# Second and third branch product of a hybrid trunk step as three rounded products each

## The chip, the core and the metric

The kernel runs on one core of one Trainium2 chip, as one program. The core has five engines that run side by side and meet through semaphores: TensorE (PE, matmul; its weight loads have a row of their own, PEld), VectorE (DVE), ScalarE (ACT), GpSimd (POOL) and SyncE (SP), whose work here is to issue DMAs. The metric is the device time of one execution in microseconds, as the median over runs of the whole program.

## What is computed

One step of a hybrid trunk for 384 tokens (128 context, 256 latent) of width 1024. Each layer normalizes and modulates the tokens, projects them, runs three branches on the projections (attention A, gated convolution B, a recurrence C), mixes them, and then runs a mixture of 64 experts. The reference, cut to the part that matters here:

```python
(qa, ka, va, u, gb, gc, qc, zf, zb, ic, oc, ga, gbr, gcr) = jnp.split(n @ lp['w_in'], split_idx, axis=-1)
o_a = attend(heads(qa), ka, va)
o_b = conv_branch(u, gb, gc, lp['w_conv'])
o_c, s_f, s_b = hgrn_branch(qc, zf, zb, ic, oc, lp['lb_f'], lp['lb_b'], lp['hgrn_g'], s0f, s0b)
mix = (jax.nn.sigmoid(ga) * (o_a @ lp['w_br_a'])
       + jax.nn.sigmoid(gbr) * (o_b @ lp['w_br_b'])
       + jax.nn.sigmoid(gcr) * (o_c @ lp['w_br_c'])) @ lp['w_out']
h = h + g1 * mix
n2 = rmsnorm(h, lp['norm2_g']) * (1 + sc2) + sh2
y = moe(n2.reshape(bsz * t, D_MODEL), lp).reshape(bsz, t, D_MODEL)
```

Each branch output is 384 x 512 and its weight 512 x 1024; all values are float32.

## The kernel before

One list, `SCHEDULE`, sets the order of the work in each engine: every engine walks the same list of stages and emits its own part of each. Semaphores between the engines do the rest. The stages run roughly in this order: norm and modulation; the input projection in units of 128 output columns (`unit`); attention between those units; the recurrence (`gates`, `decays`, `sums`, `ops`, `level`, `carry`); its outputs (`hout`, `ho_sq`, `ho_norm`, `hout_t`), with the first four branch products between them; the other 20 branch products (`branches`); the output projection (`wout`); the second norm; router, shared expert and table; and last the routed experts in a loop, 40 units here.

**Branch products.** There are 24, numbered i = 0 to 23: 8 for each branch (`br, j = i // KD, i % KD`). Product i gives 128 output columns for all 384 tokens, transposed, from 4 blocks of 128 inputs. It is made by `product` (line 1614), which emits 4 f32 matmuls with the weight block as the stationary operand (128x128) and the branch output as the moving one (128x384). An f32 matmul leaves two records in the trace, so a product leaves 8. The sources are `OA` (branch A), `GB` (B) and `OCT` (C). Products 0 to 3 stand between the recurrence's output stages, and `branches` runs 4 to 23. The results go to PSUM banks in turn, six of them from product 8 on, and TensorE waits only for the taking of product i - 6.

**Takings.** VectorE takes product i out of PSUM and multiplies it by its gate (`G`, line 1383); for branches B and C it then adds it to the sum of the first (line 1386). At i = 8 it first does three small additions for the gate rows (lines 1374 to 1376). The output projection waits for the last addition (`mix_done`).

**Recurrence outputs.** For m = 0 to 2 ScalarE copies the output (`hout`, line 863), VectorE sums its squares (lines 1340 to 1342), ScalarE takes a root (line 870), VectorE scales (lines 1068 to 1072, 1349), TensorE transposes (`hout_t`, line 1823) and VectorE writes `OCT` (line 1361).

**Weights.** SyncE streams them through a ring of three slots (`bigA`). The three branch weights have a slot each; the two halves of the output weights follow when the products of branch A and of branch B are done (lines 593 and 603).

**Rounded products.** The input projection already works with the form that the change uses. ScalarE copies a weight piece to a rounded high part (`split`, line 789, of 128x2048; `split_g`, line 781, of 128x1024), VectorE subtracts it from the whole and writes the low part over the weight in the ring (lines 1173 and 1142), and TensorE makes high x high, high x low and low x high (lines 1664 to 1666 and 1676 to 1678). A rounded matmul leaves one record. A unit has 8 blocks and 24 such matmuls, and ScalarE takes it at line 763.

**Memory.** `GB`, `OCT`, `KEY`, `QC` and `Z` are stretches of one tile, `bigB`; `nT` holds the low part of the normalized tokens (`NLO`) until the last unit. GpSimd clears the rows that the expert gathers will fill, a memset of 128x2048 on `bigB` (line 1017), when `ho_ready` says that the recurrence's outputs are in PSUM; the gathers come after the second norm.

## Time and profile before

| | us |
|---|---|
| median of the runs | 1142.43 |
| lowest and highest of three runs | 1141.66, 1144.81 |
| profiled execution, its own time | 1142.93 |
| its span in the trace | 1141.0 |
| TensorE busy | 1077.7 (94%) |
| VectorE busy | 449.1 (39%) |
| ScalarE busy | 296.3 (26%) |
| GpSimd busy | 131.4 (12%) |

The profile is one execution, recorded on the chip. Its times count from the span's start; the own time is what the device reports for that execution, 1.9 us more than the span. Busy time of TensorE counts pipelined matmuls with their modelled ends, so their durations overlap; how fast matmuls follow each other is read from the distance between starts, or from when another engine takes the results. "Idle before" and what stands behind the arrow say how long the engine had nothing to do ahead of an instruction and which work ended that.

### The profile page before, as it was taken

What the parts mean: (1) busy time and instruction counts of PE and PEld (TensorE: products, weight loads), DVE (VectorE), ACT (ScalarE), POOL (GpSimd) and SP (SyncE); (2) the same over time, 40 slices, a digit from 0 to 9 for tenths busy, and PEclk for the clock granted to TensorE, in tenths of its full rate; (3) what the DMA queues carried; (4) which work ended last, traced back from release to release, by engine and by line L of the source; (5) the groups of instructions that cost most, each with busy time, mean ns of one, the idle gap of its engine ahead of it and who ended that gap; (6) DMA issues with size and microseconds to landing.
All of it is one profiled execution on the core that took longest, in us unless ns stands there. A gap on an engine that the chain in (4) does not pass through costs nothing.

```text
span 1141.0 us, 14556 instructions
## 1 busy us (share of the span) xinstructions
PE 1077.7 (94%) x4704; PEld 671.6 (59%) x4704; DVE 449.1 (39%) x1046; ACT 296.3 (26%) x439; POOL 131.4 (12%) x142
## 2 busy tenths in 40 slices
PE   4999999998999988999999999999999999999985
PEld 2499988787888985554645444444444444444432
DVE  2233544355789837334641212211212212211247
ACT  3334443337444444001321111111111111111101
POOL 0020321000000000000015111121111121121100
PEclk9999999999999999999998999999999999999998
DMA  9999875447444333540239999999999999999683
GB/s 355 398 257 371 118 96 87 149 166 269 176 149 148 149 135 92 179 147 1 93 161 413 369 394 385 404 395 377 385 414 391 378 380 409 408 394 387 257 357 156
DMA packets 88527, 306.60 MB, mean 269 GB/s; under 512 B 13398, under 2 KB 17750, under 8 KB 66464
## 3 DMA queue, kind: packets, MB, share of 16 engines
q1 hardware_dynamic: 68896, 270.63, 60.6%
q0 software_dynamic: 12256, 26.80, 10.2%
q10 hardware_dynamic: 7328, 8.55, 2.2%
q8 instruction: 29, 0.48, 0.2%
q14 instruction: 18, 0.15, 0.0%
HBM read 285.31 MB, written 36.85 MB: 282 GB/s over the span
## 4 chain that ended last, share of the span: by engine, by line
PE 35%; DMA 20%; issue 4%; DVE 4%; ACT 1%; POOLq 1%; POOL 0%; ACTq 0%; DVEq 0%
DMA y_parts<-bigB,IDX 17%; PE PS L1614 10%; PE PS L1951 6%; PE PS L1953 4%; PE PS L1968 3%; DMA bigB<-n_rows,IDX 3%; PE PS L1937 2%; PE PS L2019 2%; PE PS L1970 2%; PE PS L1908 1%; PE PS L2027 1%; PE PS L1676 1%; PE PS L1678 0%; PE PS L1677 0%; PE PS L1986 0%
## 5 line engine op out<-in xcount | busy, mean ns | idle before, releaser
L1951 PE MATMUL PS<-bigB 128*128 128x512 f32 x224 | 103.9, 608 | 0.0
L1664 PE MATMUL PS<-bigB_r 128*128 128x384 f32 x288 | 98.7, 343 | 3.2 <-ACT bigB L763 1.9
L1666 PE MATMUL PS<-bigB_r,bigA_r 128*128 128x384 f32 x288 | 96.5, 335 | 0.0
L1665 PE MATMUL PS<-nT_r,bigB_r 128*128 128x384 f32 x288 | 96.3, 334 | 0.0
L1953 PE MATMUL PS<-bigA,bigB 128*64 128x512 f32 x208 | 94.8, 598 | 0.0
L1954 PE MATMUL PS<-bigB 128*64 128x512 f32 x208 | 94.8, 598 | 0.0
L1951 PE MATMUL PS<-bigA,bigB 128*128 128x512 f32 x208 | 94.6, 597 | 0.0
L1551 DVE TENSOR_SCALAR bigB<-PS,bigD 128x1024 f32<-128x1024 f32 x40 | 51.3, 1283 | 101.5 <-PE PS L1968 68.9
L939 ACT ACTIVATE bigB<-PS 128x1024 f32<-128x1024 f32 x40 | 41.0, 1025 | 158.4 <-PE PS L1937 158.4
L1173 DVE TENSOR_TENSOR bigA_r<-bigA,bigB_r 128x2048 fp32r<-128x2048 f32 x18 | 41.3, 2292 | 98.2 <-ACT bigB_r L789 98.1
L1529 DVE TENSOR_TENSOR bigB<-bigB,PS 128x256 f32<-128x256 f32 x40 | 16.9, 421 | 158.1 <-ACT bigB L943 158.1
L1012 POOL DMA_INDIRECT bigB<-n_rows,IDX x27 | 27.4, 1016 | 407.1 <-issue 376.7
L1951 PEld LDWEIGHTS PS<-bigB 128*128 128x128 f32 x224 | 41.4, 194 | 42.5 <-issue 42.5
L1678 PE MATMUL PS<-bigC_r,bigA_r 128*128 128x384 f32 x192 | 65.0, 338 | 0.0
L763 ACT ACTIVATE bigB<-PS 128x384 f32<-128x384 f32 (+1 forms) x55 | 27.3, 497 | 144.3 <-PE PS L1666 70.8
L1090 DVE TENSOR_REDUCE bigD<-PS 128x1 f32<-128x2 f32 (+1 forms) x58 | 9.2, 158 | 139.1 <-PE PS L1623 122.2
L1664 PEld LDWEIGHTS PS<-bigB_r 128*128 128x128 f32 x288 | 54.0, 188 | 9.6 <-ACT bigB L763 3.7
L1951 PEld LDWEIGHTS PS<-bigA,bigB 128*128 128x128 f32 x208 | 37.6, 191 | 37.3 <-issue 37.3
L1614 PE MATMUL PS<-bigA,bigB 128*128 128x512 f32 x120 | 52.9, 596 | 3.4 <-ACT bigB L933 2.2
L1665 PEld LDWEIGHTS PS<-nT_r,bigB_r 128*128 128x128 f32 x288 | 54.1, 188 | 0.0
L1666 PEld LDWEIGHTS PS<-bigB_r,bigA_r 128*128 128x128 f32 x288 | 54.0, 188 | 0.0
L1953 PEld LDWEIGHTS PS<-bigA,bigB 128*64 128x64 f32 x208 | 26.3, 136 | 46.3 <-issue 44.5
(352 smaller groups left out, 1901.3 us busy)
## 6 DMA issues: line engine op xcount, KB each, us to landing
bigA<-in_w_in SPq DMA_DIRECT2D x17, 2048.0 KB, 11.7
bigB<-in_w_gate SPq DMA_DIRECT2D x27, 1024.0 KB, 9.3
bigB<-in_w_up SPq DMA_DIRECT2D x27, 1024.0 KB, 12.5
bigB<-in_w_down SPq DMA_DIRECT2D x27, 1024.0 KB, 12.6
bigA<-in_w_gate SPq DMA_DIRECT2D x26, 1024.0 KB
bigA<-in_w_up SPq DMA_DIRECT2D x26, 1024.0 KB
bigA<-in_w_down SPq DMA_DIRECT2D x26, 1024.0 KB, 11.0
bigA<-in_w_ada SPq DMA_DIRECT2D x8, 2048.0 KB, 10.0
```

What stands on the lines that cost most here:

```text
L939: nc.scalar.activation(XT[:, b, :, :].rearrange("p (a k) t -> p a (k t)", a=2), PS[:, 0:2, :], ACT.Copy).then_inc(xt_done, 1)
L1173: nc.vector.tensor_tensor(low, w, WHI[:, i % 2, :, :].bitcast(F32), ALU.subtract).then_inc(wlo_done, 1)
L1551: nc.vector.tensor_scalar(YS[:, p % 2, :].rearrange("p (a n) -> p a n", a=2), PS[:, 6:8, :], WC[:, p:p + 1], None, ALU.mult).then_inc(ys_d ...
L1614: last = mm(out, lhs(k), rhs(k), start=(k == 0), stop=(k == n - 1))
L1664: mm(out, wh, nh, start=(k == 0), stop=False)
L1665: mm(out, wh, nl, start=False, stop=False)
L1666: last = mm(out, wl, nh, start=False, stop=(k == KD - 1))
L1678: last = mm(out, low[:, k, :], NHI2[:, k, :], start=False, stop=(k == KD - 1))
L1951: last = mm(PS[:, 2 + b, :], XT[:, b, k, :], GU_W[s][:, :, k, :], start=first, stop=stop)
L1953: mm(PS[0:HALF, 2 + b, :], XT[:, b, k, 0:HALF], GU_W[2][:, :, k, :], start=first, stop=stop)
L1954: last = mm(PS[HALF:P, 2 + b, :], XT[:, b, k, HALF:P], GU_W[3][:, :, k, :], start=first, stop=stop)
L1968: last = mm(PS[:, 6 + hf, :], HT[:, b, k, :], DN_W[s][:, k, cols], start=(k == 0), stop=(k == 1))
```

## The change

The 16 products of branches B and C are made from rounded parts: 12 rounded matmuls each in place of 4 f32 ones. Products 0 to 7 and the output projection stay f32. The operands are split as follows.

- Sources: ScalarE copies `GB` and `OCT` (128x1536 each) to `SRC_H`, in `nT`; VectorE writes the low part over the source itself (`SRC_L`).
- Weights: each of the two branch weights is split in four pieces of 4 x 256 columns (two products each), 8 pieces in all. ScalarE copies a piece to `BRH`, over `KEY`, `QC` and `Z` (pieces 0 to 6) and over `GB`'s place (piece 7, which waits for all 16 products of branches A and B); VectorE writes the low part over the piece in the ring.
- `LATE_LOW_AT` says after which product's taking VectorE makes which low part. The stage `late_high` places ScalarE's copies.
- GpSimd's memset on `bigB` now waits for all 24 products, since pieces 3 and 4 lie there.

```diff
+LATE = ([("src", 1)] + [("br", i) for i in range(4)] + [("src", 2)] + [("br", i) for i in range(4, 8)])
+LATE_LOW_AT = {4: [("src", 1), ("br", 0)], 5: [("br", 1)], 6: [("br", 2)], 7: [("br", 3)], 9: [("src", 2)],
+               10: [("br", 4)], 12: [("br", 5)], 14: [("br", 6)], 16: [("br", 7)]}
...
-    s += [("carry_t",), ("late_sig",), ("carry_products",), ("br", 0), ("br", 1), ("hout", 0), ("brm", 0), ("brm", 1),
+    s += [("carry_t",), ("late_sig",), ("late_high", "src", 1), ("carry_products",), ("br", 0), ("br", 1), ("hout", 0), ("brm", 0), ("brm", 1),
...
-    s += [("late_act", b) for b in range(3)]
-
-    s += [("gates_out",), ("branches",), ("mod2",), ("wout", 0, 0), ("wout", 0, 1), ("norm2", 0), ("wout", 1, 0),
+    s += [("late_high", "br", 0), ("late_high", "br", 1), ("late_act", 0), ("late_act", 1), ("late_high", "br", 2),
+          ("late_high", "br", 3), ("late_high", "src", 2)] + [("late_high", "br", i) for i in range(4, 7)]
+    s += [("late_act", 2), ("gates_out",), ("late_high", "br", 7), ("branches",), ("mod2",), ("wout", 0, 0), ("wout", 0, 1), ("norm2", 0), ("wout", 1, 0),
...
+        SRC_H = [None, cut(nT_r, 0, (4, T)), cut(nT_r, 4 * T, (4, T))]
+        SRC_L = [None, cut(bigB_r, 15360, (4, T)), cut(bigB_r, 13824, (4, T))]
+        BRH = [cut(bigB_r, 16896 + 1024 * i, (4, 2 * P)) for i in range(7)] + [cut(bigB_r, 15360, (4, 2 * P))]
...
+        def late_part(key):
+
+            kind, i = key
+            if kind == "src":
+                return (GB, OCT)[i - 1], SRC_H[i], SRC_L[i]
+            cols = slice(i % 4 * 2 * P, (i % 4 + 1) * 2 * P)
+            at = SLOT_OF["br", 1 + i // 4] % NSLOT * 4096
+            whole, low = (t[:, at:at + 4096].rearrange("p (k n) -> p k n", k=4) for t in (bigA, bigA_r))
+            return whole[:, :, cols], BRH[i], low[:, :, cols]
...
+                elif st == "late_high":
+                    kind, i = ev[1:]
+                    if kind == "src":
+                        if i == 1:
+                            act.wait_ge(unit_ready, len(UNITS))
+                            act.wait_ge(conv_done, 4)
+                        else:
+                            act.wait_ge(hot_taken, NT)
+                        whole, high, _ = late_part(ev[1:])
+                        nc.scalar.activation(high, whole, ACT.Copy).then_inc(late_high, 1)
+                    else:
+                        arrived(act, ("br", 1 + i // 4))
+                        act.wait_ge(kh_done, 4)
+                        if i >= 3:
+                            act.wait_ge(ho_ready, NT)
+                        if i == 7:
+                            act.wait_ge(br_ready, 2 * KD)
+                        whole, high, _ = late_part(ev[1:])
+                        nc.scalar.activation(high, whole, ACT.Copy).then_inc(late_high, 1)
...
-            pool.wait_ge(ho_ready, NT)
+            pool.wait_ge(br_ready, 3 * KD)
             link(nc.gpsimd.memset(bigB[:, 19968:22016], 0.0))
...
+                        for key in LATE_LOW_AT.get(i, ()):
+                            whole, high, low = late_part(key)
+                            dve.wait_ge(late_high, LATE.index(key) + 1)
+                            nc.vector.tensor_tensor(low, whole, high.bitcast(F32), ALU.subtract).then_inc(late_low, 1)
...
-                        src = (OA, GB, OCT)[br]
-                        product(PS[:, br_bank(i), 0:T], lambda k: w[:, k, j * P:(j + 1) * P], lambda k: src[:, k, :], 4).then_inc(br_ready, 1)
+                        out = PS[:, br_bank(i), 0:T]
+                        if br == 0:
+                            product(out, lambda k: w[:, k, j * P:(j + 1) * P], lambda k: OA[:, k, :], 4).then_inc(br_ready, 1)
+                            continue
+                        piece = (i - KD) // 2
+                        _, high, low = late_part(("br", piece))
+                        pe.wait_ge(late_low, LATE.index(("src", br)) + 1)
+                        pe.wait_ge(late_low, LATE.index(("br", piece)) + 1)
+                        cols = slice(j % 2 * P, (j % 2 + 1) * P)
+                        for k in range(4):
+                            mm(out, high[:, k, cols], SRC_H[br][:, k, :], start=(k == 0), stop=False)
+                            mm(out, high[:, k, cols], SRC_L[br][:, k, :], start=False, stop=False)
+                            last = mm(out, low[:, k, cols], SRC_H[br][:, k, :], start=False, stop=(k == 3))
+                        last.then_inc(br_ready, 1)
```

How the instructions stand on three engines, before and after. TensorE before, from product 2 to the output projection: line 1614 is `product`, 1823 the transposes of the recurrence's output; `bigD` is `OA`'s tile, `bigB` that of `GB` and `OCT`, `bigA` the weights (and, with 512 columns, the output weights).

```order
L1614 MATMUL PS<-bigD,bigA 128x384 x4
L1823 MATMUL PS<-K,bigC 128x128 x4
L1614 MATMUL PS<-bigD,bigA 128x384 x4
L1823 MATMUL PS<-K,bigC 128x128 x4
L1614 MATMUL PS<-bigD,bigA 128x384 x16
L1614 MATMUL PS<-bigB,bigA 128x384 x64
L1614 MATMUL PS<-bigA,bigB 128x512 x32
```

TensorE after, from product 3 into product 8 (1656 and 1865 are the old 1614 and 1823):

```order
L1656 MATMUL PS<-bigD,bigA 128x384 x4
L1865 MATMUL PS<-K,bigC 128x128 x4
L1656 MATMUL PS<-bigD,bigA 128x384 x16
L1893 MATMUL PS<-nT_r,bigB_r 128x384
L1894 MATMUL PS<-bigB_r 128x384
L1895 MATMUL PS<-nT_r,bigA_r 128x384
L1893 MATMUL PS<-nT_r,bigB_r 128x384
L1894 MATMUL PS<-bigB_r 128x384
L1895 MATMUL PS<-nT_r,bigA_r 128x384
```

The 64 f32 matmuls of products 8 to 23 have become 64 triples like these; nothing else on TensorE moved.

VectorE before, products 4 to 9: line 1383 is a taking, 1386 the addition, 1374 to 1376 the gate rows.

```order
L1383 TENSOR_TENSOR bigB<-PS,bigB 128x384 x4
L1374 TENSOR_TENSOR csil<-csil 128x64
L1375 TENSOR_TENSOR csil<-csil 128x32
L1376 TENSOR_TENSOR csil<-csil 128x32
L1383 TENSOR_TENSOR bigB<-PS,bigB 128x384
L1386 TENSOR_TENSOR bigB<-bigB 128x384
```

VectorE after, products 4 to 7 (line 1421 is the taking, 1430 a low part):

```order
L1421 TENSOR_TENSOR bigB<-PS,bigB 128x384
L1430 TENSOR_TENSOR bigB_r<-bigB,nT_r 128x1536
L1430 TENSOR_TENSOR bigA_r<-bigA,bigB_r 128x4x256
L1421 TENSOR_TENSOR bigB<-PS,bigB 128x384
L1430 TENSOR_TENSOR bigA_r<-bigA,bigB_r 128x4x256
L1421 TENSOR_TENSOR bigB<-PS,bigB 128x384
L1430 TENSOR_TENSOR bigA_r<-bigA,bigB_r 128x4x256
L1421 TENSOR_TENSOR bigB<-PS,bigB 128x384
L1430 TENSOR_TENSOR bigA_r<-bigA,bigB_r 128x4x256
L1412 TENSOR_TENSOR csil<-csil 128x64
```

Ten low parts have come in, five of them ahead of product 8's taking and five behind later ones.

ScalarE before, from the last root of the recurrence's output to the gate rows (line 886 is the sigmoids of `G` for branches B and C):

```order
L870 ACTIVATE small<-small 128x4
L878 DMA csil<-ada_rows 128x8x16
L881 DMA bigC<-ada_rows 128x8x8 x2
L882 DMA bigB<-in_x 128x3x1024
L883 DMA csil<-in_b_gate 128x16
L886 ACT_TABLE_LOAD
L886 ACTIVATE bigB<-bigB 128x3072 x2
L891 DMA gate_rows<-csil 64x2x16 x2
L895 DMA bigC<-gate_rows 128x4096
```

ScalarE after, from that root's successor on (924 a piece's high part, 915 a source's, 905 the sigmoids, 929 and 933 the gate rows):

```order
L924 ACTIVATE bigB_r<-bigA 128x1024 x2
L897 DMA csil<-ada_rows 128x8x16
L900 DMA bigC<-ada_rows 128x8x8 x2
L901 DMA bigB<-in_x 128x3x1024
L902 DMA csil<-in_b_gate 128x16
L905 ACT_TABLE_LOAD
L905 ACTIVATE bigB<-bigB 128x3072
L924 ACTIVATE bigB_r<-bigA 128x1024 x2
L915 ACTIVATE nT_r<-bigB 128x1536
L924 ACTIVATE bigB_r<-bigA 128x1024 x3
L905 ACTIVATE bigB<-bigB 128x3072
L929 DMA gate_rows<-csil 64x2x16 x2
```

Two high parts stand ahead of the DMA issues now, six between the sigmoids, one behind the gate rows; a tenth (source 1) stands earlier, right behind the Silu of `late_sig`.

## Rows read from the trace of the kernel before

**Rows 1.** The chain that ended last, 420 to 610 us: start, us, what

```profile
442.30 1.58 DVE small L1342
...
451.92 53.31 PE PS L1614 x160
...
506.46 27.73 PE PS L1614 x64
```

**Rows 2.** Timeline of TensorE: start, us, engine, line, out<-in, count, idle before

```profile
445.97 0.66 PE L1823 MATMUL PS<-K,bigC 128*128 128x128 f32 x4 [1.40 <-DVE bigC L1349]
...
451.29 0.63 PE L1823 MATMUL PS<-K,bigC 128*128 128x128 f32 x4 [2.08 <-DVE bigB L1361]
451.76 12.18 PE L1614 MATMUL PS<-bigD,bigA 128*128 128x384 f32 x32
463.77 41.44 PE L1614 MATMUL PS<-bigB,bigA 128*128 128x384 f32 x128
```

**Rows 3.** Groups by line and form: count, busy us, mean ns

```profile
L1614 PE MATMUL PS<-bigB,bigA 128*128 128x384 f32 x128 | 41.4, 486 | 0.0
```

**Rows 4.** Timeline of ScalarE in the input projection: takings of rounded units

```profile
243.30 0.49 ACT L763 ACTIVATE bigB<-PS 128x384 f32<-128x384 f32 x1 [1.86 <-PE PS L1666]
247.46 0.49 ACT L763 ACTIVATE bigB<-PS 128x384 f32<-128x384 f32 x1 [3.67 <-PE PS L1666]
```

**Rows 5.** Lines 1142, 1173 (low parts), 781, 789 (high parts): min/median/max ns, starts, forms

```profile
L1142 DVE TENSOR_TENSOR bigA_r<-bigA,bigB_r x12: 1197/1216/1225, 284.7 to 415.0; 128x1024 fp32r<-128x1024 f32 x12
L1173 DVE TENSOR_TENSOR bigA_r<-bigA,bigB_r x18: 2291/2292/2294, 64.7 to 260.8; 128x2048 fp32r<-128x2048 f32 x18
L781 ACT ACTIVATE bigB_r<-bigA x12: 1048/1051/1054, 281.5 to 413.9; 128x1024 fp32r<-128x1024 f32 x12
L789 ACT ACTIVATE bigB_r<-bigA x18: 1903/1908/1920, 62.8 to 258.9; 128x2048 fp32r<-128x2048 f32 x18
```

**Rows 6.** Timeline of VectorE over the branch products

```profile
456.23 0.56 DVE L1383 TENSOR_TENSOR bigB<-PS,bigB 128x384 f32<-128x384 f32 x1 [2.23 <-PE PS L1614]
...
463.97 0.56 DVE L1383 TENSOR_TENSOR bigB<-PS,bigB 128x384 f32<-128x384 f32 x1 [2.02 <-PE PS L1614]
464.45 0.21 DVE L1374 TENSOR_TENSOR csil<-csil 128x64 f32<-128x64 f32 x1
...
466.65 0.56 DVE L1383 TENSOR_TENSOR bigB<-PS,bigB 128x384 f32<-128x384 f32 x1 [1.53 <-PE PS L1614]
467.24 0.56 DVE L1386 TENSOR_TENSOR bigB<-bigB 128x384 f32<-128x384 f32 x1
...
505.25 0.56 DVE L1383 TENSOR_TENSOR bigB<-PS,bigB 128x384 f32<-128x384 f32 x1 [1.43 <-PE PS L1614]
```

**Rows 7.** Timeline of ScalarE and its DMA queue (ACTq) around the recurrence's output

```profile
430.24 1.48 ACT L859 ACTIVATE bigD<-bigD 128x1536 f32<-128x1536 f32 x1
434.31 0.60 ACT L863 ACTIVATE bigC<-PS 128x512 f32<-128x512 f32 x1 [2.58 <-PE PS L1810]
...
449.99 0.51 ACTq L883 DMA_DIRECT2D csil<-in_b_gate  x1
...
472.43 0.35 ACTq L895 DMA_DIRECT2D bigC<-gate_rows  x1
```

**Rows 8.** GpSimd's timeline, and line 1342: min/median/max ns

```profile
442.05 1.80 POOL L1017 MEMSET bigB<- 128x2048 f32 x1 [193.31 <-PE PS L1815]
...
L1342 DVE TENSOR_SCALAR small<-small x3: 169/169/1572, 436.4 to 447.4; 128x4 f32<-128x4 f32 x3
```

**Rows 9.** SyncE's DMA issues in time; DMAs by line: KB each, us to landing

```profile
465.79 19.20 SPq L603 DMA_DIRECT2D bigA<-in_w_out  x2
...
586.40 0.37 SPq L637 DMA_DIRECT2D bigB<-in_w_gate  x1
...
bigA<-in_w_out SPq DMA_DIRECT2D x2, 2048.0 KB, 8.7
...
bigC<-gate_rows ACTq DMA_DIRECT2D x1, 2048.0 KB, 9.8
```

**Rows 10.** Busy time of engines in stretches: PE, PEld, DVE, ACT, POOL, granted clock, DMA

```profile
451.76:454.00 2.24, 2.24 (x6) 1.24 (x5) 1.87 (x5) 2.23 (x2) 0.00 (x0) 0.52 1.00 408
...
458.00:463.77 5.77, 5.77 (x19) 3.39 (x18) 1.12 (x2) 0.00 (x0) 0.00 (x0) 1.00 0.00 0
```

More of the change, by code:

```diff
@@ L455, in trunk @@
         mix_done = sem("mix_done")
+        late_high = sem("late_high_parts_ready")
+        late_low = sem("late_low_parts_ready")
         wo_ready = sem("out_products")
```

## The prediction, made before the changed kernel was run

> **What bounds the kernel now.** I read the chain that ended last first, then TensorE's own list between 427 and 550 us, then VectorE, ScalarE and GpSimd over the same stretch, and last the rows that give prices. The whole program is a chain of stages in which TensorE is nearly always the busy one; what counts is which wait ends last in the stage that is edited. The reader is to see three things.
>
> First, from 451.8 us to the output projection the chain is TensorE alone: 160 records without a break, then the output projection [rows 1]. They are 20 branch products (4 of the first branch, 8 of the second, 8 of the third); each f32 matmul leaves two records. The 16 products that are edited start at 463.77 us [rows 2], and VectorE takes one every 2.58 us: product 7 is taken at 463.97 and product 23 at 505.25, (505.25 - 463.97) / 16 = 2.58 [rows 6]. VectorE is idle 2.02 us before the taking at 463.97 and 1.53 us before that at 466.65, with "PE PS L1614" as what ended the wait [rows 6]: TensorE sets the pace.
>
> Second, a rounded product has a price in this trace. The input projection does the same three rounded matmuls per block of 128, with 8 blocks for an output: ScalarE takes such units at 243.30 and 247.46 us, 4.16 us for 24 matmuls, 0.1733 us each [rows 4]. The f32 record in the branches comes every 2.58 / 8 = 0.3225 us.
>
> Third, one row ahead of this stage is odd. The small instruction L1342 has a median of 0.169 us, and once it took 1.572 us [rows 8]. It began at 442.30, inside GpSimd's memset of 442.05 to 443.85, and ended with it [rows 1, 8]. This row is on the chain. The change moves just that memset.
>
> **The change part by part.**
>
> TensorE. Removed: 16 products of 4 f32 matmuls, 16 x 2.58 = 41.3 us [rows 3, 6]. Added: 16 products of 12 rounded matmuls, 12 x 0.1733 = 2.08 us each, 33.3 us [rows 4]. All of it is on the chain, so **-8.0 us**. The shapes are those of the row (128x128 weights, 384 columns), and the clock was granted in full in both places, so I take the row itself. The Trainium skill ("FP8 and Floating Point Precision", section TensorE Precision Notes) says that true FP32 is four passes through the array; three rounded products against four passes would be a quarter less, 10.3 us and not 8.0. The trace does not agree with passes of equal length: 0.1733 us for a rounded matmul against 0.161 us for a quarter of an f32 one.
>
> GpSimd's memset. It now waits for all 24 products instead of the recurrence's output, so it leaves 442 us and starts when product 23 is done. L1342 falls back to 0.17 us. Behind it stand ScalarE's root, VectorE's scaling, the transposes at 445.97 (1.40 us idle ahead of them, ended by DVE L1349) and, through VectorE's order, those at 451.29 [rows 2], ahead of product 4. TensorE has been idle since 444.57, just when the transposes would be released. So the whole 1.572 - 0.169 = **-1.4 us** should come through. At its new place the memset (1.80 us) runs beside VectorE's last taking and last addition, both tensor_tensor; these end the wait of the output projection. What would it cost there? Bounds: nothing, and 1.8 us if both are held to its end. During the old memset the only other VectorE row was a reduction of 0.69 us, not stretched, so the trace does not decide for tensor_tensor; I take nothing. The Trainium skill ("SBUF — State Buffer", section Who interferes with whom) says that a tensor_scalar in its two-port mode and a GpSimd instruction block each other, while a VectorE instruction with two SBUF inputs contends only with a GpSimd instruction that reads SBUF; a memset only writes. By that rule the 1.572 us row is explained and the new place is free. Gathers into the cleared rows come some 90 us later, so the late memset holds nobody up.
>
> VectorE's low parts: 8 of 128x1024 and 2 of 128x1536. The first have a row, 1.216 us, and 128x2048 is 2.292 [rows 5]; between them 1536 elements make 1.75 us. Together 8 x 1.22 + 2 x 1.75 = 13.3 us. Beside them stand 4 takings of 0.59, 16 pairs of 1.18 (twice the 0.59 from 466.65 to 467.24) and 0.7 us for three small additions like the one at 464.45 [rows 6]: 35.2 us in all. From product 4's taking to the last one TensorE gives 3 x 2.58 + 33.3 = 41.0 us. They fit, with 5.8 us over. The order matters more than the sum. With all times 1.4 us earlier than before: taking 4 at 454.8, low parts of source 1 and piece 0 done at 458.4, product 8 wants both at 462.4. Product 7 is taken at 462.6, its low part done at 464.4, gate rows at 465.1, so product 8 is taken at 465.1 instead of 464.7. Source 2's low part, after product 9, is done at about 470; product 16 starts at 479. Piece 7, after product 16, is done at about 484; product 22 starts at 491.5. Six PSUM banks let TensorE run five products ahead of the takings, so VectorE's lag of 0.4 to 1 us is covered: **0 us**.
>
> ScalarE's high parts: a copy of 128x1024 is 1.05 us, of 128x2048 1.91 [rows 5], so 1536 is about 1.5. Source 1 stands right before the first copy of the recurrence's output. The Silu ahead of it ends at 431.7 and that copy is released at 434.31 [rows 7]: the new one ends at 433.2, with 1.1 us to spare. The cover gone, it would delay the chain by what is over. Pieces 0 and 1 (2.1 us) stand before five DMA issues on ScalarE's queue; these wait 2.1 us longer. The last was issued at 449.99 [rows 7] and goes at about 450.7 now; VectorE wants what they bring at about 464, and even 2 MB land in 9.8 us [rows 9]: covered. Piece 7 has to stand behind the DMA of the gate rows, issued at 472.43 [rows 7], and behind product 15 (479), so that is when it runs; the gate rows land 9.8 us after their issue [rows 9], wanted at about 504.
>
> SyncE. The second half of the output weights is issued when product 15 is done, 484.99 before [rows 9], about 479 now; landed 8.7 us later [rows 9], wanted at about 500. What follows (shared expert, router, routed experts) is released by instructions of this chain, not by a clock of its own: the first routed weights are issued at 586.40 [rows 9], behind the table of rounds. So it shifts as a whole.
>
> **Sum.** -8.0 - 1.4 = -9.4 us. The profiled execution had 1142.93 us (span 1141.0); it would be 1133.5. The median of the runs is 1142.43, so **1133.0 us**.
>
> **Rivals.**
>
> The clock. From 451.76 to 454 us TensorE was granted 0.52 [rows 10], so 1.2 GHz for nearly all of it, after three idle stretches between products (two of them in [rows 2]). Product 4 was taken 4.5 us after 451.76 instead of 2.6 [rows 2, 6], a loss of about 1.8 us. One of the stretches, 1.40 us, goes. If that keeps the clock up the time is 1131.2. Against it: the longest, 2.08 us, stays, with the same product before it. 0.13.
>
> The memset collides with the last taking and addition: 1.8 us back, 1134.8. 0.10.
>
> A wait inside the stage, at product 8, 16 or 18, for a high or low part: ScalarE does its sigmoid of 2.8 us and five issues between pieces 1 and 2. If VectorE stood until they came and TensorE with it, 2 to 4 us would go, some 1136. 0.08.
>
> The gain is given back in the routed part, where DMA and TensorE are both full: half of it would be 1137.7, all of it 1142. Against it: nothing there starts at a fixed time. 0.07.
>
> Passes of equal length (a rounded matmul at a quarter of the f32 one, 0.161 us): 16 x 12 x 0.161 = 30.9, gain 10.4 + 1.4, 1130.6. That is what the FP32 rule of the Trainium skill would give. 0.02.
>
> Slower: VectorE becomes the bound. Its low parts stand between takings; with 21.9 us of other work in a stretch of 41.0 + 9.4 = 50.4 us, the kernel is slower than before once they cost more than 28.5 us, 2.1 times the rows. At 2.5 times (33.3 us) it is 4.8 us slower, 1147.2. What could do it is a slow form: in place, four strips of 256 columns, where [rows 5] has eight of 128 or 256. Against it: the spread there is 1197 to 1226 ns. 0.05.
>
> **How the numbers follow.** The forecast itself has 0.55. The range of 1130.5 to 1137.0 takes in the forecast with a run's own scatter (the three runs lie within 3.2 us), the clock, the memset, the equal passes and most of the waits, some 0.85; the give-back and the slower case are left out. What this kernel's measurement can tell from no change is some 0.3%, 3.4 us: faster by more means below 1139.0. Forecast, clock, memset, waits, equal passes and half of the give-back make 0.91; I say faster 0.88, same 0.07, slower 0.05, the rest being for what I have not seen.
>
> **What would show it.** Rounded matmuls at the new lines 0.173 us apart and takings of products 9 to 23 2.08 us apart; no L1342-like row of 1.5 us; GpSimd's memset at about 496 with the last addition still 0.56 us long; low parts of 1.22 and 1.75 us; the output projection from 497 instead of 506.46 [rows 1], the routed weights at about 577. It would be wrong if TensorE is idle ahead of a second- or third-branch product for a low part, or if takings are 2.4 us apart or more.

## The result and the profile after

The changed kernel has a median of 1130.98 us (four runs, 1126.82 to 1134.91), the kernel before 1142.05 (1141.27 to 1144.81). The ratio is 0.9898, 95% interval [0.9856, 0.9941], so 11.6 us or 1.0% faster. On the median of before, 1142.05, that is 1130.4 us: 2.6 us under the forecast of 1133.0 and 0.1 us under the low end of its range, 1130.5. That 0.1 us is far below what these few runs can tell: the forecast's own ratio, 1133.0 / 1142.43 = 0.9917, lies inside the interval. What shows an error in the forecast is the profile, not the total. The profiled execution had 1134.91 us, span 1132.8.

A span of this kernel varies by a few us from run to run. So I compare five stretches, cut at four instructions that both traces have: the first carry transposes, the third hout transposes ([rows 2]: 451.29 before), the first output projection ([rows 1]: 506.46) and the issue of the first routed weights ([rows 9]: 586.40).

| us | start to carry | to third hout transposes | to output projection | to routed weights | to the end |
|---|---|---|---|---|---|
| before | 421.72 | 29.57 | 55.17 | 79.94 | 554.60 |
| changed | 423.82 | 28.18 | 45.48 | 81.13 | 554.19 |

The gain lies in the second and third of them: -1.39 and -9.69, together -11.08 us. The forecast was -9.4. The front part, 2.1 us later, is not the change's: a later run of the changed kernel has 421.93, and one of the kernel before 425.47.

The chain that ended last, changed kernel (start, us, what), answers [rows 1]:

```profile
444.40 0.18 DVE small L1380
...
452.63 10.32 PE PS L1656 x32
...
496.27 0.57 DVE bigB L1421
496.87 0.57 DVE bigB L1424
497.48 27.73 PE PS L1656 x64
```

L1342 is now L1380, and takes 0.18 us where it took 1.58. TensorE alone still makes the chain up to the last taking and addition. The output projection starts at 497.48 instead of 506.46.

TensorE's timeline (start, us, engine, line, out<-in, count, idle before), answers [rows 2]:

```profile
452.00 0.63 PE L1865 MATMUL PS<-K,bigC 128*128 128x128 f32 x4 [2.09 <-DVE bigB L1399]
452.46 10.49 PE L1656 MATMUL PS<-bigD,bigA 128*128 128x384 f32 x32
462.49 0.63 PE L1893 MATMUL PS<-nT_r,bigB_r 128*128 128x384 f32 x1
```

The row of 32 records (products 4 to 7) is 10.49 us long; in [rows 2] it is 12.18. These products are not edited: this is the clock. The second hout transposes have no idle before them any more (1.40 before), the third still have 2.09.

The same groups by line and form, 452 to 500 us (count, busy us, mean ns), and the stretches of products 4 to 7 and of the rounded ones (us, then busy time of PE, PEld, DVE, ACT, POOL, the granted clock, DMA share), answer [rows 3, 10]:

```profile
L1893 PE MATMUL PS<-nT_r,bigB_r 128*128 128x384 f32 x64 | 21.7, 339 | 0.0
...
452.46:454.70 2.24, 2.24 (x9) 1.34 (x8) 1.86 (x5) 2.23 (x2) 0.00 (x0) 1.00 0.90 366
454.70:462.49 7.79, 7.79 (x26) 4.58 (x25) 6.66 (x8) 7.79 (x8) 0.00 (x0) 1.00 0.21 81
462.49:495.60 33.11, 33.11 (x192) 32.98 (x191) 24.61 (x40) 2.84 (x2) 0.00 (x0) 1.00 0.61 218
```

From the second of the 192 rounded matmuls (462.96) to the last (495.90) there are 190 steps in 32.94 us: 0.173 us each, and TensorE is busy all the time. The 339 ns of a row is twice that since neighbouring matmuls overlap; the distance between starts is what counts. The first line of stretches is the other surprise: clock 1.00 where [rows 10] has 0.52.

VectorE (timeline) and GpSimd, answer [rows 6, 8]:

```profile
455.25 0.56 DVE L1421 TENSOR_TENSOR bigB<-PS,bigB 128x384 f32<-128x384 f32 x1 [0.54 <-PE PS L1656]
455.72 1.75 DVE L1430 TENSOR_TENSOR bigB_r<-bigB,nT_r 128x1536 fp32r<-128x1536 f32 x1
457.38 1.22 DVE L1430 TENSOR_TENSOR bigA_r<-bigA,bigB_r 128x1024 fp32r<-128x1024 f32 x1
458.52 0.55 DVE L1421 TENSOR_TENSOR bigB<-PS,bigB 128x384 f32<-128x384 f32 x1
...
465.18 0.56 DVE L1421 TENSOR_TENSOR bigB<-PS,bigB 128x384 f32<-128x384 f32 x1
...
494.19 0.56 DVE L1421 TENSOR_TENSOR bigB<-PS,bigB 128x384 f32<-128x384 f32 x1 [0.93 <-PE PS L1895]
...
496.27 0.56 DVE L1421 TENSOR_TENSOR bigB<-PS,bigB 128x384 f32<-128x384 f32 x1 [0.93 <-PE PS L1895]
496.87 0.56 DVE L1424 TENSOR_TENSOR bigB<-bigB 128x384 f32<-128x384 f32 x1
...
496.30 1.80 POOL L1055 MEMSET bigB<- 128x2048 f32 x1 [246.42 <-PE PS L1895]
```

Takings are 2.08 us apart (494.19, 496.27), each after an idle of 0.93 us that ends with the product. The memset at 496.30 covers taking and addition, and both stay at 0.56 us.

ScalarE and its DMA queue, then SyncE's queue, answer [rows 7, 9]:

```profile
433.73 1.47 ACT L915 ACTIVATE nT_r<-bigB 128x1536 fp32r<-128x1536 f32 x1
436.40 0.60 ACT L882 ACTIVATE bigC<-PS 128x512 f32<-128x512 f32 x1 [1.21 <-PE PS L1852]
...
450.90 0.51 ACTq L902 DMA_DIRECT2D csil<-in_b_gate  x1
...
479.71 1.06 ACT L924 ACTIVATE bigB_r<-bigA 128x1024 fp32r<-128x1024 f32 x1 [15.44 <-DMA bigC<-gate_rows]
...
578.61 0.37 SPq L656 DMA_DIRECT2D bigB<-in_w_gate  x1
```

Source 1's high part ends at 435.20, and 1.21 us are left before the copy of the recurrence's output.

### The profile page after: what moved, and what is told of

Read it like the earlier page. It is cut to its first block, busy times and chain, and to the rows that moved or that the text cites. A ratio compares the mean times of both kernels' runs of the same rounds, so it can differ in the third digit from the quotient of the medians.

```text
span 1132.8 us, 14730 instructions
## 1 busy us (share of the span) xinstructions
PE 1071.7 (95%) x4768; PEld 682.9 (60%) x4768; DVE 459.7 (41%) x1056; ACT 306.3 (27%) x449; POOL 131.1 (12%) x142
## 4 chain that ended last, share of the span: by engine, by line
PE 38%; DMA 18%; issue 4%; DVE 3%; ACT 1%; POOLq 1%; POOL 0%; ACTq 0%; DVEq 0%
DMA y_parts<-bigB,IDX 16%; PE PS L2005 7%; PE PS L1656 6%; PE PS L2007 5%; PE PS L2022 4%; DMA bigB<-n_rows,IDX 2%; PE PS L1991 2%; PE PS L2073 2%; PE PS L1962 2%; PE PS L2024 2%; PE PS L1893 1%; PE PS L1895 1%; PE PS L1894 1%; PE PS L2081 1%; PE PS L1718 1%
```

## Experiments

What is concluded below rests on two things: the ratio to before, and the stretches between the same instructions in the profile. "S2" is from the carry transposes to the third hout transposes (29.57 before), "S3" from there to the output projection (55.17 before). None of the kernels leaves work out; some add work that nobody reads.

### The change again, and its two halves

**e1_again**: the changed kernel, word for word.

> The changed kernel once more, for a tighter size. Parts read from its first trace: the products save 8.0 us, the memset's stall 1.4 us, and product 4 came 1.7 us sooner because the TensorE clock did not fall there. Theory A (two parts of the change and a clock that falls at random places): 9.4 us faster than before in the long run, and up to 11.1 if the fall at product 4 is always gone. Theory B (more is gained later in the program): over 11.1 us. In its profile product 4 is taken 2.7 to 2.8 us after it starts if the clock holds, 4.5 if it falls.

Measured: 1133.45 us, ratio 0.9908 [0.9888, 0.9928]; S2 28.17, S3 45.49. The two places of the gain repeat to 0.01 us in the profile, and the gain itself within the intervals.

**e2_memset_moved**: the kernel before, with one wait of GpSimd changed.

```diff
-            pool.wait_ge(ho_ready, NT)
+            pool.wait_ge(br_ready, 3 * KD)
```

> The kernel before, with one edit: GpSimd's memset waits for all 24 products. Theory A: L1342 has no long row, the output projection starts 1.4 us sooner, the kernel is 1.4 us faster; if the shorter idle stretch also keeps TensorE's clock up at product 4, 3.1 us. Rival (the memset holds VectorE's last taking and addition at its new place): the last addition is longer than 0.56 us and up to 1.8 us are lost again, no change in the time.

Measured: 1139.12 us, ratio 0.9967 [0.9950, 0.9984]; S2 28.17, S3 53.47. TensorE's timeline:

```profile
444.49 0.66 PE L1823 MATMUL PS<-K,bigC 128*128 128x128 f32 x4
449.81 0.63 PE L1823 MATMUL PS<-K,bigC 128*128 128x128 f32 x4 [2.09 <-DVE bigB L1361]
450.28 10.49 PE L1614 MATMUL PS<-bigD,bigA 128*128 128x384 f32 x32
```

So one wait alone gives 1.40 us at the stall and 1.70 us more where nothing was edited, at products 4 to 7, 10.49 instead of 12.18. The timed runs agree: 0.9967 is 3.8 us, interval 1.8 to 5.7, more than the stall's 1.4 alone. The clock belongs to the memset's half of the change, not to the rounded products.

**e3_memset_also_early**: the changed kernel with a second memset at the old place, so the rounded products alone; the later high parts and the late memset wait for the early one.

```diff
+            pool.wait_ge(ho_ready, NT)
+            nc.gpsimd.memset(bigB[:, 19968:22016], 0.0).then_inc(zeroed, 1)
             ...
```

> The changed kernel with the memset done twice: once at its old place, when the recurrence's outputs are there (ScalarE's high parts 3 to 7 wait for it), and once at its new one. This is the rounded products alone. Theory A: the small tensor_scalar behind the recurrence's second output is 1.57 us long again, 1.4 us slower than the changed kernel, 8.0 us faster than before; if the idle stretch it makes is what lets the clock fall at product 4, 3.1 us slower than the changed kernel. Rival (the memset has no part in it): as the changed kernel.

Measured: 1137.5 us, ratio 0.9949 [0.9919, 0.9978]; S2 29.57, S3 47.18. TensorE's timeline:

```profile
452.80 12.18 PE L1660 MATMUL PS<-bigD,bigA 128*128 128x384 f32 x32
```

The stall is back to the hundredth, the products' row is 12.18 us again, and the rounding alone is worth 55.17 - 47.18 = 7.99 us. With the clock held (e2 to e1) it is 53.47 - 45.49 = 7.98. The term of 8.0 us stands either way.

**e4_low_twice**: the changed kernel with each low part preceded by an equal one into an unused strip.

```diff
+                            link(nc.vector.tensor_tensor(junk, whole, high.bitcast(F32), ALU.subtract))
```

> The changed kernel with each of the ten low parts on VectorE preceded by one of the same shape into cells that nothing reads, so that a low part costs twice, 26.6 us in all. By a walk through the waits from the trace's durations: TensorE starts to wait from product 12 on and the last addition ends 5.6 us later than in the changed kernel. By the sum in the prediction alone (48.5 us of VectorE work against 41.0 us of TensorE) 7.5 us. If VectorE's work is hidden well beyond what I think: no change.

Measured: 1139.73 us, ratio 0.9973 [0.9957, 0.9989]; S3 49.04, so only 3.6 us more than 45.48; the sum had wanted 7.5 and the walk through the waits 5.6. VectorE's timeline:

```profile
457.03 0.56 DVE L1421 TENSOR_TENSOR bigB<-PS,bigB 128x384 f32<-128x384 f32 x1 [0.54 <-PE PS L1660]
...
500.55 0.55 DVE L1421 TENSOR_TENSOR bigB<-PS,bigB 128x384 f32<-128x384 f32 x1
501.14 0.56 DVE L1424 TENSOR_TENSOR bigB<-bigB 128x384 f32<-128x384 f32 x1
501.62 0.55 DVE L1421 TENSOR_TENSOR bigB<-PS,bigB 128x384 f32<-128x384 f32 x1
502.20 0.56 DVE L1424 TENSOR_TENSOR bigB<-bigB 128x384 f32<-128x384 f32 x1
```

From 457.03 on no row has idle before it: VectorE is the bound. First to last taking is 44.6 us, against 41.0 in the changed kernel (455.25 to 496.27), and that is the 3.6 us. My sum of rows was too high: it made the changed kernel's work, without the added parts, 35.2 us, and 48.5 with them. The starts show where: 500.55, 501.14, 501.62, so an addition starts 0.59 us after its taking, but the next taking 0.48 us after the addition; I had put 0.59 for both. In the changed kernel a low part starts 0.47 us after its taking (455.25, 455.72), and the next taking 1.14 us after a low part of 1.22 (457.38, 458.52). That is 0.1 us at some 40 places. The added parts take 13.6 us here from start to start (eight of 1.25 and two of 1.79), so I estimate that the changed kernel asks 44.6 - 13.6 = 31.0 us of 41.0 of VectorE in that stretch.

### What holds the clock at product 4

Three kinds of reasons were possible: TensorE's idle time ahead of the product, GpSimd's memset itself, or chance. In the tables and below, "fell" means products 4 to 7 as in the profile of before (12.18 us), "held" 10.49 us.

**f1_filled_gap**: the kernel before, with idle f32 matmuls on constants ahead of the second hout transposes, where the stall leaves 1.40 us.

```diff
+                    if m == 1:
+                        pe.wait_ge(br_taken, 1)
+                        for _ in range(2):
+                            mm(PS[:, 2, 0:T], ident, kc(K_SCAN), start=True, stop=True)
```

> The kernel before, memset at its old place, with two idle f32 matmuls (1.29 us, into a bank that nobody reads then) ahead of the second transposes of the recurrence's output, where TensorE is idle for 1.40 us. Theory A (that idle stretch is what lets the clock fall at product 4): the stall of L1342 stays, from the carry transposes to the third output transposes 29.57 us as before; product 4 comes 2.8 us after its start and not 4.5; from the third output transposes to the output projection 53.47 us and not 55.17. The kernel is 1.7 us faster than before. Rival (the fall comes with the memset or by chance): 55.17 us and no change.

Measured: 1143.01 us, ratio 0.9994 [0.9981, 1.0007]; S2 29.57, S3 55.17. TensorE's timeline:

```profile
443.62 1.45 PE L1822 MATMUL PS<-K 128*128 128x384 f32 x4
445.19 0.66 PE L1827 MATMUL PS<-K,bigC 128*128 128x128 f32 x4
450.51 0.63 PE L1827 MATMUL PS<-K,bigC 128*128 128x128 f32 x4 [2.09 <-DVE bigB L1361]
450.97 12.18 PE L1614 MATMUL PS<-bigD,bigA 128*128 128x384 f32 x32
```

The stretch is filled and the clock falls all the same. (The timed runs don't decide: their interval holds both no change and the 0.9985 that was expected.) "The 1.40 us of idle lets the clock fall" does not hold.

**g1_delay_no_memset**: e2 (no memset there), with a VectorE reduction in the place of the stall.

```diff
+                    if m == 1:
+                        link(nc.vector.tensor_reduce(small[:, 84:85], K[:, 0:1200], AX.X, ALU.add))
```

> The kernel before, with the memset moved behind the last branch product (as in the run that moved it alone), and in its place one VectorE reduction of 1200 elements ahead of the second mean of squares, which is to last 1.3 to 1.6 us, as the memset's stall did (1.572 for 0.169). No work is left out; the reduction is added and nobody reads it. Theory A, that the third transposes' lateness itself decides the clock at product 4: the stretch from the carry transposes to the third hout transposes is 29.5 us again instead of 28.17, and the stretch from there to the output projection 55.17 instead of 53.47; the kernel is at 0.996 to 1.002 of before. Rival B, that the memset on GpSimd (or VectorE's being blocked) and not the lateness goes with the fall: 29.5 and then 53.47, and 0.997 to 0.999 of before. In either the first stretch shows whether the delay was made.

Measured: 1141.71 us, ratio 1.001 [0.9994, 1.0025]; S2 29.62, S3 55.17. VectorE, then TensorE:

```profile
443.47 1.40 DVE L1343 TENSOR_REDUCE small<-K 128x1 f32<-128x1200 f32 x1
...
452.50 0.63 PE L1825 MATMUL PS<-K,bigC 128*128 128x128 f32 x4 [2.09 <-DVE bigB L1363]
452.96 12.18 PE L1616 MATMUL PS<-bigD,bigA 128*128 128x384 f32 x32
```

GpSimd has no row here, and everything that the stall cost is back, the clock included: e2's whole gain is gone. The lateness (the third hout transposes come 1.4 us later than in e2) is enough, without the memset.

**g2_fill_third**: the kernel before, memset and stall in place, with the 2.08 us ahead of the third hout transposes filled.

```diff
+                    if m == 2:
+                        pe.wait_ge(ho_taken, 2)
+                        for _ in range(3):
+                            mm(PS[:, 4, 0:T], ident, kc(K_SCAN), start=True, stop=True)
```

> The kernel before, with three f32 matmuls of 384 columns of constants ahead of the third hout transposes, in the 2.08 us in which TensorE is idle there; the earlier fill of the 1.40 us stretch left product 4 at 55.17. No work is left out. Theory A, that this idle stretch, the last and longest before the product, lets the clock fall: the stretch to the output projection is 53.47 instead of 55.17, and the kernel is 1.5 to 1.9 us faster than before (0.9983 to 0.9987), or as much less as the fill is in the way (at most 0.3 us). Rival C, that the clock falls for what came earlier, the whole stage's idle share: it stays 55.17, and the kernel is at 1.000.

Measured: 1143.25 us, ratio 1.0016 [0.9999, 1.0033]; S2 29.57, S3 53.47. TensorE's timeline:

```profile
447.09 0.66 PE L1827 MATMUL PS<-K,bigC 128*128 128x128 f32 x4 [1.40 <-DVE bigC L1349]
...
450.17 2.10 PE L1822 MATMUL PS<-K 128*128 128x384 f32 x6
452.42 0.63 PE L1827 MATMUL PS<-K,bigC 128*128 128x128 f32 x4 [0.15 <-DVE bigB L1361]
452.88 10.49 PE L1614 MATMUL PS<-bigD,bigA 128*128 128x384 f32 x32
```

In this profile the clock held although the stall was there. But the timed runs show no gain: 0.9985 was expected and the interval excludes it. One profile and ten times disagree, and I can't say why; this experiment is not a proof.

**g4_before_look** and **h2_after_third** are the two kernels word for word, for more profiles of the same place.

> The kernel before, word for word, for one more profile. If what it does before product 4 decides the clock there, the stretch from the third hout transposes to the output projection is 55.17 again, as in the three profiles that had the 1.4 us stall. If it is chance, there is one chance in some that it is 53.47. No work is left out.

> The changed kernel word for word, beside the one above, on the same chip. The stretch from the third hout transposes to the output projection is 45.48 for the third time if the 1.4 us less of idle before it hold the clock; 47.2 if the two earlier profiles were chance. The ratio is 0.989 to 0.992, as before. No work is left out.

Measured: g4 1144.24 us (one run), S2 29.57, S3 55.17; h2 1132.57 us, ratio 0.9923 [0.9902, 0.9944], S2 28.16, S3 45.48. All profiles together (idle of TensorE ahead of the first, second and third hout transposes):

| kernel | idle, us | products 4 to 7 |
|---|---|---|
| before, g4, e3 | 1.70, 1.40, 2.08 (g4 2.09) | clock fell, 3 of 3 |
| g1 (delay, no memset) | 1.70, 1.44, 2.09 | clock fell |
| f1 (second filled) | 1.70, -, 2.09 | clock fell |
| g2 (third filled) | 1.70, 1.40, 0.15 | held |
| e2, changed, e1, h2, e4 | 1.70, -, 2.08 or 2.09 | held, 5 of 5 |

With the lateness and nothing filled the clock fell in 4 of 4 profiles; without the lateness it held in all 5 of this table. It is not chance and not the memset. It is not the idle time alone either: f1 and e2 have the same idle stretches and differ in the result. They differ in when the stretches come, 1.4 us later in f1, and in the four filling records.

The three kernels filled elsewhere, below, show a second condition. f2 and g3 are as late as the kernel before or later (S2 30.60 and 29.61), and the clock held at product 4; ahead of the third hout transposes only 0.48 and 0.15 us were idle there. With g2 these are 3 of 3 late profiles in which that stretch was short and the clock held (in f2 it had fallen and come back just before). So in the 14 profiles it fell where both came together, the lateness and some 2.08 us idle ahead of the third hout transposes (5 of 5), and held where either was missing (9 of 9). Where it fell, it was still granted in full during that stretch, and went to 0.50 only 0.5 to 1.1 us after the third hout transposes had begun: in the profile of before they begin at 451.29, and the clock is 1.00 until 451.75 and 0.50 from 452.00. Why the two have to come together stays open.

### Can the clock be held elsewhere

The profile of the changed kernel shows the clock below 1.00 also at 200 to 220 and 280 to 300 us, at idle stretches of 2.66 and 3.04 us.

**f2_after_filled**: the changed kernel with these two filled.

```diff
+                        if h == NH - 1 and u == 2:
+                            ...
+                            for _ in range(10):
+                                mm(PS[:, (n + 1) % 2, 0:P], ident, ident, start=True, stop=True)
...
+                            if i == 1:
+                                for _ in range(4):
+                                    mm(PS[:, 3, 0:T], ident, kc(K_SCAN), start=True, stop=True)
```

> The changed kernel with idle f32 matmuls in two longer idle stretches of TensorE: ten of 128 columns (2.2 us) in the 2.66 us ahead of the last head's third score near 205 us, and four of 384 columns (2.6 us) in the 3.04 us ahead of the second gate unit near 286 us. The clock is at half rate behind both in every trace of the changed kernel. Theory A (idle stretches cost the clock): it is 1.00 in both places, the carry transposes start up to 3.4 us sooner than 423.5 to 423.8 us, and the kernel is up to 3.4 us faster than the changed kernel. Rival (the fillings delay the real work, or the clock falls anyway): as the changed kernel or slower by up to 0.5 us a place.

Measured: 1129.62 us, ratio 0.9874 [0.9856, 0.9893]; the clock is 1.00 at both filled places, and the carry transposes start at 421.32 (423.82, 423.45 and 421.93 in the three profiles of the changed kernel). But S2 is 30.60. ScalarE and its queue, and 5 us stretches of the same columns as above:

```profile
433.91 2.48 ACTq L885 DMA_DIRECT2D out_new_state<-bigC  x2
436.42 1.28 ACT L889 ACT_TABLE_LOAD   x1 [1.92 <-issue]
...
435.00:440.00 5.00, 1.78 (x15) 1.58 (x15) 2.61 (x9) 1.97 (x3) 0.00 (x0) 0.87 0.35 98
440.00:445.00 5.00, 5.00 (x25) 5.00 (x25) 3.36 (x10) 0.21 (x1) 0.00 (x0) 0.50 0.00 0
```

ScalarE issues the two DMAs of the state ahead of the table load for the root. They took 2.48 us here, and 0.95 in the profiles of before, of the changed kernel and of all runs so far. The root came late, TensorE stood 3.22 us instead of 1.70, and then it ran at 0.50, that is 1.2 GHz, from 440 to 445.

**g3_after_filled_4**: f2 with the stretches ahead of the first and the third hout transposes filled too.

```diff
+                    if m == 0:
+                        for _ in range(2):
+                            mm(PS[:, 0, 0:T], ident, kc(K_SCAN), start=True, stop=True)
+                    if m == 2:
+                        pe.wait_ge(ho_taken, 2)
+                        for _ in range(3):
+                            mm(PS[:, 4, 0:T], ident, kc(K_SCAN), start=True, stop=True)
```

> The changed kernel with four stretches filled by f32 matmuls of constants: the two before (about 205 and 286 us) and those ahead of the first and of the third hout transposes (1.70 and 2.08 us). No work is left out. With two filled it ran at 0.9874 of before [0.9856, 0.9893], but the granted clock fell to 0.97 and 0.86 at 420 to 460 us. Theory A, that idle stretches there let it fall: the clock is 1.00 from 400 to 480 us, the stretch from the carry transposes to the third hout transposes is 28.2 instead of 30.6, and the ratio is 0.984 to 0.987. Rival C, that the stage is too thin as a whole, whatever is filled: the fall stays and the ratio is 0.987 to 0.989, the fills costing up to 0.3 us.

Measured: 1129.55 us, ratio 0.9899 [0.9882, 0.9916]; S2 29.61, S3 45.48, clock 1.00 from 400 to 480. The fall is gone, as the theory wanted. The expectation of 28.2 was missed: the issues took 2.39 us again, and that delay of 1.4 us stays whatever is filled (1.85 us were still idle ahead of the first hout transposes). The ratio missed too: theory A wanted 0.984 to 0.987, which lies outside the interval, so no further gain is shown over f2.

**h1_state_later**: the changed kernel with three stretches filled (those of f2 and the third hout transposes'), and the two issues moved behind the root; the diff shows the move.

```diff
                     nc.scalar.activation(OS[m], PS[:, HO_BANK[m], :], ACT.Copy).then_inc(ho_taken, 1)
-                    if m == 0:
-                        for d in range(2):
-                            act.dma_start(new_state[d].rearrange("h k v -> k h v"), STC[:, d, :, :]).then_inc(state_out, 16)
...
                     nc.scalar.activation(small[:, 36:40], small[:, 32:36], ACT.Sqrt).then_inc(ho_root, 1)
+                    if m == 0:
+                        for d in range(2):
+                            act.dma_start(new_state[d].rearrange("h k v -> k h v"), STC[:, d, :, :]).then_inc(state_out, 16)
```

> The changed kernel with three stretches filled (about 205 us, 286 us, and the 2.08 us ahead of the third hout transposes), and with the two issues of the state's DMAs on ScalarE moved from ahead of the first head-norm root to behind it. In the two filled runs so far the issues took 2.39 and 2.48 us where they take 0.95 in all ten other profiles, and TensorE waited 3.2 us ahead of the first hout transposes (1.70 otherwise); in one of them the clock then fell for 10 us. No work is left out. Theory A, that the late root, not the fills themselves, made those stretches: the stretch from the carry transposes to the third hout transposes is 28.2 us whatever the issue takes, the clock is 1.00 from 420 to 480 us, and the ratio to before is 0.984 to 0.987, 1.5 to 3 us under the kernel with two filled (0.9874) . Rival B, that the issues are now in the way of ScalarE's next copies by as much: 28.2 to 29.7, and 0.986 to 0.989.

Measured: 1129.83 us, ratio 0.9897 [0.9877, 0.9917]; S2 28.16, S3 45.48. The changed kernel in the same comparison (h2) has 1132.57 and 0.9923. ScalarE's timeline and queue, then the stretches:

```profile
434.80 1.28 ACT L886 ACT_TABLE_LOAD   x1
436.47 0.21 ACT L886 ACTIVATE small<-small 128x4 f32<-128x4 f32 x1 [0.38 <-DVE small L1380]
436.48 0.95 ACTq L889 DMA_DIRECT2D out_new_state<-bigC  x2
...
420.00:440.00 20.00, 17.88 (x120) 14.91 (x119) 11.43 (x26) 13.47 (x14) 0.00 (x0) 1.00 0.39 132
440.00:460.00 20.00, 19.85 (x78) 12.30 (x77) 17.19 (x38) 13.61 (x14) 0.00 (x0) 1.00 0.32 86
```

The table load no longer stands behind the issues, S2 is the expected 28.2 and the clock stays up. The ratio was missed: 0.9897 is above the 0.984 to 0.987 of theory A, which lies outside the interval, and above the 0.986 to 0.989 of rival B as well. The stretch speaks for theory A; the gain that it was to bring in the whole time is not there. Since the issues took 0.95 us here, the case in which they take long was not seen. The three filled kernels have medians of 1129.6, 1129.6 and 1129.8 us, the changed kernel in its three comparisons 1131.0, 1133.5 and 1132.6. They lie 0.1 to 0.3% under it; in the one comparison that has both, h1 and h2, the intervals overlap, so I call that likely and not shown.

How far single spans scatter with the clock can be read from 171 runs of these kernels (all but g4's). With one level for each kernel and a common slope on the mean granted clock, a run is 0.94 us longer for each 0.001 that its clock is lower (standard error 0.05), and 1.4 us of scatter are left. Compared at equal clock, the changed kernel is 9.5 +- 0.9 us faster (two standard errors; h2 10.3 +- 1.2) and e2 2.5 +- 0.9. The first is about the forecast's -9.4, the sum without the clock's term. It is no proof to a microsecond: the same fit gives e3 6.4 +- 1.0, where its profile shows 7.99, and e2 more than the stall's 1.4. Nor do the timed runs of the changed kernel decide for a gain of 9.4 or of 11.1 us: its three ratios, weighted by their intervals, give some 9.9 +- 1.6 us. The clock's term is shown by the profiles.

## Why the prediction was wrong in size, step by step

- **The rounded products, -8.0.** Right: -7.99 in e3, -7.98 between e2 and e1. The row of another stage, 0.1733 us per rounded matmul or 2.08 per product, held here: takings are 2.08 us apart. The rival of equal passes (0.161 us each) wanted 1.93. The Trainium skill ("FP8 and Floating Point Precision", section TensorE Precision Notes) tells of four passes for true FP32; this trace does not bear out a rounded product at the price of one of four.
- **The stall, -1.4.** Right: S2 29.57 to 28.18, and e2, e3 and g1 switch it off and on. That the late memset costs nothing at its new place was right too: taking and addition beside it stay at 0.56 us. The Trainium skill ("SBUF — State Buffer", section Who interferes with whom) lets GpSimd block a tensor_scalar in its two-port mode, and a VectorE instruction with two SBUF inputs only where GpSimd's own instruction reads SBUF, which a memset does not; the traces agree on both sides, 1.572 us against 0.169 for L1342 [rows 8], and 0.56 us for L1424 after the change.
- **The clock: the failed step.** The sum left it out and I put it as a rival at 0.13, with the reason "the longest, 2.08 us, stays, with the same product before it". It was worth -1.70 us, 12.18 against 10.49 for the unedited products 4 to 7. The price in that rival, 1.8, was nearly right, the chance was not. The argument took the longest idle stretch ahead of the product for the one that decides. In the runs that stretch was the same, 2.08 or 2.09 us, in 5 profiles that fell and in 5 that held, so by itself it decides nothing (that it matters together with the lateness, g2, f2 and g3 suggest); and I gave 1.4 us less of lateness a small chance where it went with the clock in 9 of 9 profiles with nothing filled. With that term the sum is -11.1, and 1142.43 - 11.1 = 1131.3.
- **The low end of the range.** 1130.5 left only 0.7 us under the clock's case, 1131.2, where three runs of one kernel lie within 3.2 us. The three comparisons of the changed kernel gave ratios of 0.9898, 0.9908 and 0.9923, on 1142.4 us 1130.8, 1131.9 and 1133.6. The first is the lowest of them, and on the 1142.05 of its own comparison it is 1130.4, just outside; the other two lie inside. That the miss is 0.1 us and not 0 is the luck of four runs; the missing clock term is what brought the forecast that near to the edge. By that scatter the range should have ended at about 1129.
- **VectorE.** 0 us, right: between the first and the last taking, 41.0 us, TensorE never waited for it. At product 8, taken at 465.18 without idle before, VectorE was behind by a low part and the gate rows, as said (product 7 had been taken at 462.99, 2.19 us before; 2.5 were forecast), and the PSUM banks covered that. The room was mis-sized: 5.8 us over by the sum, 10.0 by e4. So VectorE would become the bound later than the slower rival had it.
- **ScalarE.** Source 1's high part left 1.21 us before the copy, 1.1 were forecast. The issues behind pieces 0 and 1 hardly waited: the last one stands at 450.90, 0.9 us later than in [rows 7], of which 0.7 is the later root ahead of them (448.30 against 447.60). Forecast were 2.1 us; that term was too high, and hidden anyway. Piece 7 ran at 479.71, as said.
- **What follows shifts as a whole.** Right within what runs show: output projection to routed weights is 79.94 before, 81.13 in two profiles of the changed kernel and 79.95 in the third; the two longer ones go with a clock of 0.91 at 540 to 560 us, and the change touches nothing there. The give-back did not come. That the output projection starts at 497.48 and the memset at 496.30, near the forecast's 497 and 496, is luck: the run's front part was 2.1 us late, and the gain up to there was 11.08 us and not 9.4.

## What to carry to other kernels

Price an edit by a row of the same shape elsewhere in the trace, at the same granted clock; here that was good to 0.02 us in 8. But when an edit also takes a microsecond or two of waiting out of a stage in which TensorE stops and starts, look at the next stretch whose granted clock is near 0.5: it may be won or lost as a whole, 1.7 us here, and such a term belongs in the sum with even odds or as two forecasts, not in a footnote. For an engine that might become the bound, count the distance between starts in a stretch where it never idles, not the lengths of its rows.

## What the runs showed of the hardware that I had not expected

- A delay alone took the clock: a VectorE reduction of 1.40 us, far from TensorE's work, made the products 10 us later 1.70 us longer (g1 against e2), with 2.09 us idle ahead of the third hout transposes in both.
- Two DMA issues on ScalarE's queue took 0.95 us in twelve profiles, and 2.48 and 2.39 in f2 and g3, which differ from the changed kernel by fills alone. What makes them long was not tried.
- VectorE is held by more than the memset. In h1, beside GpSimd's tensor_tensor rows, a VectorE one of 192 elements took 2.45 us, where the next of the same line took 0.34, and a copy of 9 elements 2.31 instead of 0.16. Both ended with GpSimd's row or up to 0.2 us behind it (607.18 against 606.96, 609.41 against 609.38). TensorE waits 2.63 us there, in the stage of the routing; that is a place to look next.

```profile
602.28 2.37 POOL L1068 TENSOR_TENSOR bigB<-bigB,bigC 128x1024 f32<-128x1024 f32 x1
604.60 2.36 POOL L1067 TENSOR_TENSOR nT<-nT,bigC 128x1024 f32<-128x1024 f32 x1
607.04 2.34 POOL L1068 TENSOR_TENSOR bigB<-bigB,nT 128x1024 f32<-128x1024 f32 x1
...
604.73 2.45 DVE L1118 TENSOR_TENSOR bigC_r<-K,bigC 128x192 fp32r<-128x192 f32 x1 [1.16 <-issue]
607.10 2.31 DVE L1119 CAST bigD_r<-bigD_r 128x9 fp32r x1
```
